# The last part of a panel's head work moved behind the next panel's eviction

## The reference

```
def rms_norm(t, gain):
    tf = t.astype(float32)
    return tf * rsqrt(mean(tf * tf, axis=-1) + EPS) * gain
def qk_prep(t, gain, cos, sin):
    return partial_rope(rms_norm(t, gain), cos, sin)
# block 0
mq, mk, mv, nq, nkv, ng = split(h @ w_in, SPARSE_SPLITS)
```

## Time and profile before

| what | value |
|---|---|
| median of 3 runs | 1767.02 us |
| profiled execution | 1764.94 us, its span 1763.1 us |
| TensorE busy | 1581.5 us (90%), 10302 matmuls |
| VectorE busy | 941.1 us (53%), 1610 instructions |
| ScalarE busy | 718.4 us (41%) |
| granted TensorE clock, mean | 0.936 |
| low half of a weight half unit, L903 | x424, mean 1215 ns |
| high half, L526 | x424, mean 1045 ns |
| eviction by VectorE, L955 | x18, mean 672 ns |
| gain, L1066 | x16, mean 938 ns |
| chain that ended last | PE 81%, DVE 12%, DMA 2%, ACT 2% |

### The profile page before, as it was taken

How to read it: one execution, slowest core, us unless ns; L and a number is a source line. 1 busy time by engine, 2 the same in 40 slices (tenths; PEclk the granted TensorE clock), 3 DMA queues, 4 the chain that set the end, 5 groups by cost and what they waited for, 6 DMA issues and landing times.

```text
span 1763.1 us, 24461 instructions
## 1 busy us (share of the span) xinstructions
PE 1581.5 (90%) x10302; PEld 1326.5 (75%) x10302; DVE 941.1 (53%) x1610; ACT 718.4 (41%) x1098; POOL 0.2 (0%) x4
## 2 busy tenths in 40 slices
PE   3966898999989888999988999889999795999997
PEld 1753586999867656998767998678988683779986
DVE  3582246444577685433467445663355786363455
ACT  1432154333444433333334554344444443345543
POOL 0000000000000000000000000000000000000000
PEclk9987798999989889999998999989999897999999
DMA  9833712885544445998752645639755342445552
GB/s 363 303 138 128 243 36 73 298 299 175 183 143 167 146 166 176 315 308 300 265 200 72 191 168 191 203 107 308 255 191 191 120 170 94 166 144 182 177 191 84
DMA packets 165844, 336.41 MB, mean 191 GB/s; under 512 B 8160, under 2 KB 109160, under 8 KB 165480
## 3 DMA queue, kind: packets, MB, share of 16 engines
q1 hardware_dynamic: 134720, 226.71, 37.5%
q10 hardware_dynamic: 31016, 108.16, 18.1%
HBM read 333.79 MB, written 1.05 MB: 190 GB/s over the span
## 4 chain that ended last, share of the span: by engine, by line
PE 81%; DVE 12%; DMA 2%; ACT 2%; issue 1%; ACTq 0%; SPq 0%; DVEq 0%
PE ps L1503 22%; PE ps L1504 21%; PE ps L1505 21%; PE ps L1475 5%; DVE wlo L903 2%; PE ps L1634 2%; DVE res L981 1%; DVE work L979 1%; PE ps L1631 1%; PE ps L1718 1%; PE ps L1668 1%; PE ps L1701 1%; DMA ring<-in_ada_w_dram 1%; ACT whi L526 1%; PE ps L1697 1%
## 5 line engine op out<-in xcount | busy, mean ns | idle before, releaser
L903 DVE TENSOR_TENSOR wlo<-wraw,whi 128x1024 fp32r<-128x1024 f32 (+1 forms) x424 | 497.8, 1215 | 413.4 <-ACT whi L526 413.1
L526 ACT ACTIVATE whi<-wraw 128x1024 fp32r<-128x1024 f32 (+1 forms) x424 | 423.1, 1045 | 479.9 <-PE ps L1505 454.0
L1503 PE MATMUL ps<-hT_hi,whi 128*128 128x256 f32 x1472 | 421.9, 287 | 0.0
L1504 PE MATMUL ps<-hT_lo,whi 128*128 128x256 f32 x1472 | 416.5, 283 | 0.0
L1505 PE MATMUL ps<-hT_hi,wlo 128*128 128x256 f32 x1472 | 416.2, 283 | 0.0
L1503 PEld LDWEIGHTS ps<-hT_hi,whi 128*128 128x128 f32 x1472 | 282.3, 192 | 20.1 <-issue 18.1
L1504 PEld LDWEIGHTS ps<-hT_lo,whi 128*128 128x128 f32 x1472 | 282.4, 192 | 0.0
L1505 PEld LDWEIGHTS ps<-hT_hi,wlo 128*128 128x128 f32 x1472 | 282.3, 192 | 0.0
L1503 PE MATMUL ps<-whi,act_hi 128*128 128x512 f32 x560 | 219.0, 391 | 0.0
L1504 PE MATMUL ps<-wlo,act_hi 128*128 128x512 f32 x560 | 218.1, 389 | 0.0
L1505 PE MATMUL ps<-whi,act_lo 128*128 128x512 f32 x560 | 217.9, 389 | 0.0
(11 more groups left out here) (200 smaller groups left out, 1377.9 us busy)
## 6 DMA issues: line engine op xcount, KB each, us to landing
wraw<-in_mlp_w_dram SPq DMA_DIRECT2D x96, 1024.0 KB, 5.2
ring<-in_ada_w_dram ACTq DMA_DIRECT2D x90, 1024.0 KB, 5.3
wraw<-in_ffn_w_gate_dram SPq DMA_DIRECT2D x22, 1024.0 KB, 6.1
wraw<-in_ffn_w_up_dram SPq DMA_DIRECT2D x22, 1024.0 KB, 5.6
wraw<-in_ffn_w_down_dram SPq DMA_DIRECT2D x22, 1024.0 KB, 4.9
wraw<-in_diff_w_in_dram SPq DMA_DIRECT2D x12, 1024.0 KB, 4.9
wraw<-in_attn_w_qkv_dram SPq DMA_DIRECT2D x12, 1024.0 KB, 5.0
wraw<-in_sp_w_in_dram SPq DMA_DIRECT2D x8, 1024.0 KB, 13.0
```

Source lines behind the costliest of these rows:

```text
L526: nc.scalar.activation(whi[:, u % 2, part], wraw[:, u % 4, part], ACT.Copy).then_inc(hi_ready, 1)
L903: nc.vector.tensor_tensor(wlo[:, u % 2, part], wraw[:, u % 4, part], whi[:, u % 2, part].bitcast(F32), ALU.subtract).then_inc(lo_ready, 1)
L1503: mm(dst, s_hi, m_hi, start=start, stop=False, skip_group_check=skip)
L1504: mm(dst, s_hi, m_lo, start=False, stop=False, skip_group_check=skip)
```

## The change

Part 3 of a head group no longer runs at step 3 of `row_segment`. It runs behind `panel_rows` and, where there is one at that place, behind `held_split`. Only VectorE's program changes; the number of its instructions and its waits stays.

```diff
             for n, w in enumerate((1024, 1024, 792)):
-                row_segment(f"in0_{n}", ada=(n == 0), heads=(lambda i: heads0(n - 1, (i,))) if n else None)
+                row_segment(f"in0_{n}", ada=(n == 0), heads=(lambda i: heads0(n - 1, range(i, min(i + 1, 3)))) if n else None)
                 panel_rows(r0, 1024 * n, w)
                 if n < 2:
                     held_split(f"in0_{n}")
+                if n:
+                    heads0(n - 1, (3,))
             heads0(2, range(4))
...
             for n in range(3):
-                row_segment(f"in1_{n}", heads=(lambda i: heads1(n - 1, i)) if n else None)
+                row_segment(f"in1_{n}", heads=(lambda i: heads1(n - 1, i) if i < 3 else None) if n else None)
                 panel_rows(r1, 1024 * n, 1024)
                 if n < 2:
                     held_split(f"in1_{n}")
+                if n:
+                    heads1(n - 1, 3)
...
             for n, (name, rows) in enumerate((("q3", q3), ("kvl", kvl))):
-                row_segment(name, heads=lambda i: heads3(n, (i,)))
+                row_segment(name, heads=lambda i: heads3(n, range(i, min(i + 1, 3))))
                 panel_rows(rows, 0, 1024)
                 if name == "q3":
                     held_split(name)
+                heads3(n, (3,))
             heads3(2, range(4))
```

## The result

The changed kernel takes 1750.19 us, the median of 4 runs (1749.27 to 1755.33), beside 1767.34 us for the kernel before (4 runs): a ratio of 0.9908, interval 0.9889 to 0.9928, which is 16.3 us by the ratio, from 12.7 to 19.6 (the two medians differ by 17.2). Its profiled execution took 1750.06 us with a span of 1748.3, 14.9 less than the one of before. The forecast was 1751.8, 15.2 us less.

The account below looks back on a forecast made before the run. VectorE's chain to the mark was taken to bound the row stages' ends, with TensorE 90% busy. Gains of 6.9, 7.0 and 1.3 us sum to 15.2, from 1767.0 to 1751.8 us; range 1748.5 to 1757.

Parts of the forecast that it names:

- VectorE's chain sets the ends: Row stages: VectorE's chain to the mark sets the end; losing idle time, marks come 6.9 us earlier in stage 0.
- B: Boundaries of stages 0 and 1: TensorE's own wait and the half clock behind it count, 6.6 us each; no chance given.
- The gate leaves the path in stage 1, with a slower clock for the transposes: End of stage 1: gate matmuls no longer set the transposes' start; gain 7.0 us, between 6.6 and 7.5.
- the two rows of 5.29 and 6.21: Time in us of 32 transposes before: 5.29 right behind the gate, 6.21 at 1477.45 behind a long wait.
- Unit 2 is fed: Behind the boundaries, TensorE gets unit 2's low half in time: 0.7 us to spare in stage 1, 0.3 wait in stage 0.
- Stage 3 gains 1.3: At kvl, the moved part 3 covers the squares VectorE waited for; gain 1.3 us, from 0.9 to 1.3.
- Rival 3, slower: Part 3 starves unit 2 in in0_2 and in1_2 and the clock stays at half; 1775.3 us, chance 4%.
- The range: Whole kernel: 1748.5 to 1757 us, with room for a mis-sized clock term, leaving out the rivals (14%).
- Nothing seen behind the row stages: Stretches behind the row stages: no term in the sum, 1 us in the forecast's own range for things not seen.

Follow-up runs that it names:

- bound_only: Kernel before with part 3 moved only at the boundaries in0_1 to in0_2 and in1_1 to in1_2; 1759.33 us, ratio 0.9951.
- ends_only: Kernel before with part 3 moved only at the last panels in0_2, in1_2 and kvl; 1770.69 us, ratio 1.0027.
- between: Changed kernel, but at the boundaries of stages 0 and 1 part 3 stands between eviction and held split; 1759.0 us, ratio 0.9951 to before.
- late_low2: Changed kernel with VectorE making the low halves of two units later in in0_2, in1_2 and kvl; 1758.39 us, ratio 0.9952 to before.
- s1_only: Kernel before with the change made in stage 1 only; 1760.45 us, ratio 0.9968.
- keep_busy: Kernel before with 15 extra unread matmuls in each of TensorE's two waits for the eviction; 1764.24 us, ratio 0.9987.
- after: First profile of the changed kernel, compared with the kernel before; median 1750.19 us, ratio 0.9908.
- late_warm2: Changed kernel with the edit of late_low2 and extra unread matmuls in TensorE's gaps ahead of the marks; 1750.52 us, ratio 0.9908 to before.
- ends_again2: ends_only unchanged, run once more for a second profile; 1761.53 us.

## Why the prediction was right

- *VectorE's chain sets the ends.* Right. Stage 0: 6.9 us forecast at the mark, 7.0 measured; stage 1: 5.1 and 5.25; stage 3: 1.3 and 1.36. bound_only, where TensorE's waits are all but gone and the chain keeps its last gap, gained 5.8 us at the mark of stage 0, what the chain said and not B's 6.6; ends_only, which leaves those waits, still gained 1.4 there.
- *The gate leaves the path in stage 1, with a slower clock for the transposes.* Right: 7.0 forecast between 6.6 and 7.5, 7.24 measured; the transposes took 5.68 us, between the two rows of 5.29 and 6.21.
- *Unit 2 is fed.* Right, without the wait of 0.3 us that I had foreseen in stage 0: the changed kernel has no wait of TensorE for L903 there.
- *Stage 3 gains 1.3.* Right in sum for a reason I had not named: 2.4 at the maxima, 1.1 given back.
- *Rival 3, slower.* It did not come, but its point was set too high. I had it decide from a wait of about 4 us; in between the clock fell behind a wait of 2.12 us, though not behind one of 2.52 us, so the length of the wait alone does not decide it. The 0.7 us to spare in stage 1 held.
- *The range.* Medians of 1750.19 and 1751.35 lie within 1.6 us of the forecast. The spread was underrated: 2 of 8 runs of the changed kernel took 1755.33 and 1756.54, with a mean clock of 0.935 for 0.938 to 0.941, and small edits near it (between, late_low2, the long runs of ends_only) cost 5 to 12 us, with mean clocks of 0.927 to 0.938. 1757 as an upper end held, with nothing to spare for single runs.
- *Nothing seen behind the row stages.* The sum put these stretches at nothing and gave no reason; the range had 1 us for them. In the changed kernel each stayed within 0.4 us up to stage 3, and that is luck: between the mark of stage 0 and its first maxima s1_only, between, keep_busy and bound_only lost 2.0 to 3.1 us, and in late_low2 the attention of stage 1 lost 10.6. The mechanism of the row stages is shown; that the whole kernel came within 1.6 us of the forecast rests on this luck as well.

## What to carry to other kernels

When an in-order engine both empties the bank that the matmuls wait for and does work that nobody waits for yet, put the emptying first, and what feeds the next tile (here the held split) before the rest too. Count such a gain on the chain that sets the stage's end: TensorE had 13 us of waits and half clock at the two boundaries here, and with those nearly gone and nothing else moved (bound_only) the two stages gained 10 and the median 7.4. Then look at the clock in the stretches behind the edit, since an edit that moved the marks by two us (late_low2) went with a loss of ten there.

## What the runs showed of the hardware

- A wait of 2.12 us of TensorE was followed by 3 us and more at granted clock 0.50 that set in after it had resumed (between, stage 1). A wait of 2.52 us in stage 0 of the same profile left it at 1.00, and so did one of 0.39 us (after). In late_warm2 it fell in a wait of 2.31 us.
- The attention of stage 1, one stream of instructions, ran at 1.00 (after, 597 to 632) or at 0.50 for 24 us in which the profile shows TensorE busy throughout (late_low2, 595 to 619), and the difference was 10.6 us of 82.
- The 32 transposes of stage 3 took 5.17 to 5.22 us in the six profiles with kvl's part 3 moved and 6.18 to 6.23 in the five without, and with the first went 1.0 to 1.1 us more behind the stage's end. Elsewhere the places of the clock's shifts do not repeat so: the transposes of stage 0 took 7.52 and 5.88 us in two profiles of one kernel (ends_only and ends_again2).
